# Three x loads on ScalarE's queue, squares behind the first roundings, small results turned inside block 3, and block 4 rounded ahead of the gates

## The chip, the cores and the metric

The kernel runs on one core of one Trainium2 chip. The metric is the time of one launch on the device in microseconds (us). The program computes a two-layer model on 256 tokens of width 1024. This case is about its first 40 us.

## What is computed

The part of the reference that the change touches is the first norm, the one large product after it, and what happens to the small columns of that product. The rest of the model (chunked attention of four kinds, feed-forward blocks, a second layer with differential attention) follows and is the same in both kernels.

```python
def rms_norm(x, g):
    xf = x.astype(jnp.float32)
    y = xf * lax.rsqrt(jnp.mean(xf * xf, axis=-1, keepdims=True) + EPS)
    return (y * g.astype(jnp.float32)).astype(x.dtype)

def token_mix(h, w_in, ...):                     # h = rms_norm(x, norm1_g)
    p = (h @ w_in).astype(jnp.float32)           # 1024 x 3612
    (fox_qkv, fox_f, gdn_qkv, gdn_b, gdn_a, gdn_z, hg_q, hg_f, hg_i, hg_g,
     gla_qk, gla_v, gla_gk, gla_g) = jnp.split(p, _cut_points(IN_SIZES), axis=-1)
    log_f = jax.nn.log_sigmoid(fox_f + fox_b_f).transpose(0, 2, 1)
    qkv = jax.nn.silu(causal_dwconv(gdn_qkv, gdn_conv_w))
    beta = jax.nn.sigmoid(gdn_b).transpose(0, 2, 1)
    g = (-jnp.exp(gdn_a_log) * jax.nn.softplus(gdn_a + gdn_dt_bias)).transpose(0, 2, 1)
    log_a = jax.nn.log_sigmoid(gla_gk @ gla_w_gk + gla_b_gk) / GLA_NORM
    ...
```

## The kernel before

**Tiling.** Activations stand channel-major: `x` is 128 partitions by 8 chunks of 128 channels by 256 tokens. All weights come as one stream of blocks of 1024 rows by 256 columns (1 MB each), into a ring of three slots, `raw`. Products are made in float32 precision from rounded parts: ScalarE rounds a block into `w_hi` (the helper `split`, called `block_hi(n)` here), VectorE writes the rest `raw - w_hi` into `w_lo` (`block_lo(n)`), and TensorE adds three products for each chunk: high by high, low weight by high operand, high weight by low operand. A block of 256 columns is therefore 48 products of 128x256, in two halves of 24 (`project(n, 0)` and `project(n, 1)`).

**Semaphores around the blocks.** `hi_ready` and `lo_ready` count rounded blocks, `raw_loaded0` to `2` the loads of a slot, `block_used` the blocks that TensorE is done with. SyncE's `weights_in(n)` waits for `lo_ready` of the block that last used the slot and issues the next load; `split` waits for the load and for `block_used`.

**The opening.** Block 0 holds the 28 small columns (gates of three heads groups and the low-rank input `gla_gk`), block 1 is `gdn_q`, block 2 `gdn_k`, block 3 `gdn_v`, block 4 `hg_q`, block 5 `fox_q`. SyncE issues all loads: for each of four quarters b the two x chunks (256 KB) and a quarter of block 1 (256 KB), with the small columns after the first; then block 2 in two halves, constants, `w_gk`, block 3, the row of biases, 1.6 MB of masks, block 4 and so on. ScalarE's `first_chunks` takes quarter by quarter: it rounds the weights (L1722), scales and rounds the two chunks into `h_hi` (L1725), and squares the two chunks (L1729). VectorE follows with the low parts (L2528, L2486), the small columns' low part (L2534), and the sums of the squares between them. TensorE warms up with 13 products of zeros (`keep_busy`), then `first_columns` does block 1 chunk by chunk, with the small columns two chunks behind: 72 products in all.

**The norm.** The products are made on the raw x; the reciprocal root `r_1` is multiplied in afterwards. `mean_of_x` is a product of ones with the summed squares, at once behind `first_columns`; ScalarE's `rstd_x` turns it into `r_1` (L1743, L1750). Then VectorE scales the small columns (L2547, `small_t`) and block 1 (L2604, `gdn_scale`). TensorE transposes the scaled small columns and multiplies by `w_gk` (`turn_small`, `gk_product`) between the halves of block 2.

**The convolution and the gates.** A gdn block is scaled by VectorE (`gdn_scale`), gets its last tap from ScalarE (`gdn_last_tap`, L1879) and three more from VectorE (`gdn_taps`, six of L2614). Gates: ScalarE copies the turned small columns (L1886) and rounds the masks (L1889), VectorE and ScalarE alternate over small tiles, and TensorE's `gates` sums them with the rounded masks behind block 3.

**What sets the order.** Every engine's program is written out by hand in one fixed order, and each queue runs in that order; nothing is scheduled at run time.

## Time and profile before

| | us |
|---|---|
| median of 3 runs | 1010.1 |
| lowest and highest | 1009.82 and 1011.12 |
| the profiled execution, whole | 1009.94 |
| its span in the profile | 1008.1 |
| TensorE busy in the span | 997.1 (99%) |
| VectorE, ScalarE, GpSimd busy | 848.4, 620.5, 9.5 |

A row of the timeline shows the start of a group of like instructions, the time from the first one's start to the last one's end, engine, source line, operation, tile written from tiles read, and in brackets how long the engine stood idle before it and what released it. A second row's start less the first's is what the first took of its engine's queue; that is used below as the pitch of an operation. Matmuls overlap, so their pitch (0.117 us for 128x256) is less than the length of one.

### The profile page before, as it was taken

Reading aid. Unit: us, or ns where it says so; the run is one execution under the profiler, and the core shown is the slowest. Engines: PE = TensorE matmul, PEld = TensorE weight load, DVE = VectorE, ACT = ScalarE, POOL = GpSimd, SP = SyncE. Lnnn points to the kernel's source line nnn. Section 1 sums busy time; section 2 is a strip of 40 time slices with the busy share of each in tenths; the row PEclk is TensorE's granted clock in tenths of the full one; section 3 lists DMA queues with packets and bytes.
Section 4 is the critical chain, followed back from the end, with each engine's and each line's share of the span. In section 5 each row is a group of like instructions: output and inputs, shape, how many; then the busy total and the mean of one; then the engine's idle time right before and its main releaser. Section 6 shows DMA issues by size and latency. Waiting matters only on the chain.

```text
span 1008.1 us, 20874 instructions
## 1 busy us (share of the span) xinstructions
PE 997.1 (99%) x8362; PEld 936.5 (93%) x8362; DVE 848.4 (84%) x1226; ACT 620.5 (62%) x858; POOL 9.5 (1%) x21
## 2 busy tenths in 40 slices
PE   8999999999999999999999999999999999999997
PEld 7999999999999998899999999999999999999996
DVE  5974896899988878879999888899776899988887
ACT  6754565657565655466666555775677676555575
POOL 0000001000000000001000000000000000000000
PEclk9999999999999999999999999999999999999999
DMA  9533315455655545566566554444444355655541
GB/s 330 179 124 97 126 44 201 165 192 187 208 190 184 196 143 204 180 235 210 199 209 209 174 203 171 165 165 170 165 147 152 126 204 205 212 178 196 184 150 42
DMA packets 26786, 177.04 MB, mean 176 GB/s; under 512 B 3261, under 2 KB 3541, under 8 KB 6368
## 3 DMA queue, kind: packets, MB, share of 16 engines
q1 hardware_dynamic: 25616, 171.31, 49.2%
q0 software_dynamic: 1104, 4.78, 1.6%
q8 instruction: 50, 0.82, 0.3%
q14 instruction: 16, 0.13, 0.0%
HBM read 175.02 MB, written 2.63 MB: 176 GB/s over the span
## 4 chain that ended last, share of the span: by engine, by line
PE 91%; DVE 4%; DMA 2%; ACT 2%; issue 1%; SPq 0%; DVEq 0%
PE PS L613 78%; PE PS L564 12%; DMA arena<-masks_in 1%; DVE w_lo L2473 1%; DMA raw<-weights 1%; DVE arena L2614 1%; DVE h_store L2486 0%; PE PS L1567 0%; DVE x L3158 0%; ACT w_hi L1662 0%; DVE arena L3390 0%; DVE arena L3152 0%; PE PS L935 0%; PE PS L903 0%; ACT arena L2043 0%
## 5 line engine op out<-in xcount | busy, mean ns | idle before, releaser
L613 PE MATMUL PS<-h_store,w_hi 128*128 128x256 f32 (+1 forms) x1840 | 475.5, 338 | 1.4 <-DVE w_lo L2528 1.2
L2473 DVE TENSOR_TENSOR w_lo<-raw,w_hi 128x2048 fp32r<-128x2048 f32 x152 | 347.9, 2290 | 50.6 <-ACT w_hi L1662 45.5
L613 PE MATMUL PS<-h_store,w_lo 128*128 128x256 f32 (+1 forms) x1400 | 365.4, 281 | 0.1
L1662 ACT ACTIVATE w_hi<-raw 128x2048 fp32r<-128x2048 f32 x154 | 294.2, 1911 | 82.6 <-PE PS L613 70.2
L613 PEld LDWEIGHTS PS<-h_store,w_hi 128*128 128x128 f32 x1840 | 303.6, 187 | 40.6 <-DVE w_lo L2528 1.7
L613 PEld LDWEIGHTS PS<-h_store,w_lo 128*128 128x128 f32 (+1 forms) x1400 | 253.2, 188 | 0.5 <-DVE h_store L3087 0.3
L613 PE MATMUL PS<-act_hi,w_hi 128*128 128x256 f32 x688 | 191.1, 280 | 0.2 <-DVE act_hi L3087 0.2
L613 PE MATMUL PS<-act_hi,w_lo 128*128 128x256 f32 x688 | 190.7, 279 | 0.1
L613 PE MATMUL PS<-act_lo,w_hi 128*128 128x256 f32 x688 | 187.6, 279 | 0.0
L613 PEld LDWEIGHTS PS<-act_hi,w_hi 128*128 128x128 f32 x688 | 129.3, 188 | 1.6 <-DVE act_hi L3087 0.6
L613 PEld LDWEIGHTS PS<-act_hi,w_lo 128*128 128x128 f32 x688 | 129.3, 188 | 0.3 <-DVE act_hi L3087 0.3
L613 PEld LDWEIGHTS PS<-act_lo,w_hi 128*128 128x128 f32 x688 | 127.5, 188 | 0.0
L2156 ACT ACTIVATE arena<-PS 128x512 f32<-128x512 f32 x51 | 30.2, 592 | 88.1 <-PE PS L613 88.1
L2148 ACT ACTIVATE arena<-arena,channel 128x256 f32<-128x256 f32 x132 | 63.6, 530 | 13.6 <-DVE arena L3235 12.4
L613 PE MATMUL PS<-w_hi,h_store 128*128 128x256 f32 (+1 forms) x368 | 71.3, 301 | 0.0
L3212 DVE SCALAR_TENSOR_TENSOR arena<-arena,channel 128x254 f32<-128x254 f32 x132 | 57.9, 480 | 7.6 <-DVE arena L3208 0.3
L613 PEld LDWEIGHTS PS<-w_hi,h_store 128*128 128x128 f32 x368 | 56.2, 188 | 2.9 <-ACT w_hi L1776 0.4
L3208 DVE SCALAR_TENSOR_TENSOR arena<-arena,channel 128x255 f32<-128x255 f32 x132 | 57.7, 479 | 1.0 <-ACT arena L2148 0.9
L3233 DVE TENSOR_TENSOR arena<-PS,arena 128x512 f32<-128x512 f32 x51 | 35.0, 686 | 20.9 <-ACT arena L2156 20.9
L613 PE MATMUL PS<-w_lo,h_store 128*128 128x256 f32 (+1 forms) x184 | 45.8, 296 | 0.4 <-DVE w_lo L2473 0.4
L564 PE MATMUL PS<-h_store,w_hi 128*128 128x256 f32 x256 | 45.4, 279 | 0.0
L564 PE MATMUL PS<-arena 64*64 64x64 f32 (+8 forms) x1356 | 41.5, 224 | 0.0
(405 smaller groups left out, 1147.1 us busy)
## 6 DMA issues: line engine op xcount, KB each, us to landing
raw<-weights SPq DMA_DIRECT2D x155, 1024.0 KB, 5.0
raw<-weights SPq DMA_DIRECT2D x12, 256.0 KB, 4.0
arena<-masks_in SPq DMA_DIRECT2D x1, 1600.0 KB, 12.2
bias_by_key<-bias_by_distance POOLq DMA_DIRECT2D x1, 1536.0 KB, 8.5
x<-x_in SPq DMA_DIRECT2D x4, 256.0 KB, 4.4
raw<-weights SPq DMA_DIRECT2D x2, 512.0 KB, 8.3
arena<-weights POOLq DMA_DIRECT2D x2, 512.0 KB, 6.1
arena<-bias_by_key POOLq DMA_DIRECT2D x1, 1024.0 KB, 6.6
```

The source lines that it names most:

```text
L564: return pe.matmul(o, lhs, rhs, start=start, stop=stop)
L613: return pe.matmul(o, lhs, rhs, start=start, stop=stop, skip_group_check=True)
L1662: act.activation(w_hi[:, slot, :], raw[:, slot, :], ACT.Copy).then_inc(hi_ready, 1)
L2148: ins = act.activation(dst[:, c, :], src[:, c, :], ACT.Identity, scale=w, bias=b)
L2156: act.activation(low, PS[:, bank:bank + 2, TOK:512], ACT.Copy).then_inc(sem("low_copied"), 1)
L2473: tt(w_lo[:, slot, :], raw[:, slot, :], w_hi[:, slot, :].bitcast(F), ALU.subtract).then_inc(lo_ready, 1)
L2614: mark(stt(dst, PS[:, bank_of_block(n), f * TOK:(f + 1) * TOK - d], ch("gdn_conv", (3 - d) * 6 + 2 * s + f), dst, ALU.mult, ALU.add))
L3208: stt(y[:, c, 1:TOK], src[:, c, 0:TOK - 1], channel[:, bass.ds(col(1) + c, 1)], y[:, c, 1:TOK], ALU.mult, ALU.add).then_inc(ready[0], 1)
L3212: ins = stt(y[:, c, 2:TOK], src[:, c, 0:TOK - 2], channel[:, bass.ds(col(0) + c, 1)], y[:, c, 2:TOK], ALU.mult, ALU.add)
L3233: tt(z, PS[:, bank:bank + 2, 0:TOK], low, ALU.add).then_inc(sem("parts_added"), 1)
```

## The change

1. **Loads.** SyncE still issues the first quarter of x. The other three are issued by ScalarE, behind its table load. The small columns are loaded behind the second weight quarter. The biases' row now counts on `ident_and_channel` (to 64), the masks alone on `mix_inputs` (to 16).
2. **Squares.** ScalarE squares the first half of x after the fourth quarter, and the second half after it has rounded block 2. VectorE's sums follow: one in front of block 2's low part, the rest behind it.
3. **First columns.** Of each chunk TensorE now does both high products, then both with the low weights, then both with the low operand, and waits for each kind by itself. The small results stand in bank 3 in place of 7.
4. **The mean** of the squares is taken inside the second half of block 2, the small columns are turned inside the first half of block 3, and `gates` moves behind the first half of block 4. Block 3 now does its low weights last, as blocks 2 and 4 to 7 did.
5. **ScalarE** rounds block 3 before `rstd_x`, and the second tap and block 4 before the masks and gates. **VectorE** takes block 3's low part ahead of the norm, scales blocks 1 and 2 together, and takes block 4's low part before the gates' arithmetic.

```diff
@@ SyncE @@
             sp.dma_start(channel[:, 0:KC], channel_in[:, 0:KC]).then_inc(sem("gains_loaded"), 16)
+            sp.dma_start(x[:, 0:2, :], x_in[:, 0:2, :]).then_inc(sem("x_loaded0"), 16)
             for b in range(4):
-                sp.dma_start(x[:, 2 * b:2 * b + 2, :], x_in[:, 2 * b:2 * b + 2, :]).then_inc(sem(f"x_loaded{b}"), 16)
...
-                if b == 0:
+                if b == 1:
                     sp.dma_start(raw[:, 0, 0:KC * SMALL], small_in).then_inc(raw_loaded[0], 16)
...
-            sp.dma_start(row[:, :], row_in.partition_broadcast(P)).then_inc(sem("mix_inputs"), 16)
+            sp.dma_start(row[:, :], row_in.partition_broadcast(P)).then_inc(sem("ident_and_channel"), 16)
@@ TensorE, first_columns @@
+                    pe.wait_ge(hi_chunk, k + 1)
+                    if k == 6:
+                        pe.wait_ge(hi_ready, 2)
...
+                    products(w_hi, h_hi, k == 0)
+                    if k == 6:
+                        pe.wait_ge(lo_ready, 2)
+                    elif k % 2 == 0:
+                        pe.wait_ge(sem("quarter_lo"), k // 2 + 1)
+                    products(w_lo, h_hi)
+                    pe.wait_ge(lo_chunk, k + 1)
+                    last = products(w_hi, h_lo, False, k == KC - 1)
@@ TensorE, project and its calls @@
-                low_last = n == 2 or 4 <= n <= 7
+                low_last = 2 <= n <= 7
...
             first_columns()
-            mean_of_x(0, 6, sum_1, True)
             project(2, 0)
-            turn_small()
-            gk_product()
-            project(2, 1)
-            project(3, 0)
+            project(2, 1, between=lambda: mean_of_x(0, 6, sum_1, True))
+            project(3, 0, between=small_parts)
             project(3, 1)
+            project(4, 0)
             gates()
-            project(4, 0)
             project(4, 1)
@@ ScalarE, first_chunks @@
-                    act.activation(sq4[:, b, :], flat(x[:, 2 * b:2 * b + 2, :]), ACT.Square).then_inc(sem("x_squares"), 1)
+                square(0)
+                square(1)
                 act.wait_ge(sem("half_loaded"), 16)
                 act.activation(w_hi[:, 2, 0:BLK // 2], raw[:, 2, 0:BLK // 2], ACT.Copy).then_inc(sem("quarter_hi"), 1)
                 act.wait_ge(raw_loaded[2], 16)
                 act.activation(w_hi[:, 2, BLK // 2:BLK], raw[:, 2, BLK // 2:BLK], ACT.Copy).then_inc(hi_ready, 1)
+                square(2)
+                square(3)
@@ ScalarE, order @@
             act.preload_act_table_set(TABLES)
+            for b in range(1, 4):
+                act.dma_start(x[:, 2 * b:2 * b + 2, :], x_in[:, 2 * b:2 * b + 2, :]).then_inc(sem(f"x_loaded{b}"), 16)
...
-            rstd_x(0, 6, (r_1, r_1_col))
...
             block_hi(3)
+            rstd_x(0, 6, (r_1, r_1_col))
             gdn_last_tap(0, 1)
+            small_copy()
+            gdn_last_tap(1, 2)
+            block_hi(4)
             gates()
             gk_logs()
-            block_hi(4)
-            gdn_last_tap(1, 2)
             block_hi(5)
@@ VectorE @@
-                if b == 2:
-                    sum_of_three(0, sum_1)
-            sum_of_last(0, sum_1)
-            fold_sum(sum_1)
+            dve.wait_ge(sem("x_squares"), 2)
+            link(tt(sum_1, sq4[:, 0, :], sq4[:, 1, :], ALU.add))
...
+            dve.wait_ge(sem("x_squares"), 3)
+            link(tt(sum_1, sum_1, sq4[:, 2, :], ALU.add))
+            sum_of_last(0, sum_1)
+            fold_sum(sum_1)
+            split(3, 3 % RING)
             dve.wait_ge(sem("x_rstd"), 1)
...
             gdn_scale(0, 1)
-            block_lo(3)
+            gdn_scale(1, 2)
+            gdn_taps(0, 1)
             gates_in()
-            gdn_taps(0, 1)
             gk_logits()
+            block_lo(4)
             gates()
             gate_parts()
             gk_logs()
-            gdn_scale(1, 2)
-            block_lo(4)
             gdn_taps(1, 2)
```

The order of instructions shows two places that matter. The first is ScalarE's queue at the opening; in it `w_hi<-raw` of 128x512 is a weight quarter, `h_store<-x` the operand, `xn<-x` a square. Before:

```order
L1857 ACT_TABLE_LOAD
L1722 ACTIVATE w_hi<-raw 128x512
L1725 ACTIVATE h_store<-x,channel 128x256 x2
L1729 ACTIVATE xn<-x 128x512
L1722 ACTIVATE w_hi<-raw 128x512
L1725 ACTIVATE h_store<-x,channel 128x256 x2
L1728 ACTIVATE w_hi<-raw 128x224
L1729 ACTIVATE xn<-x 128x512
```

And with the change:

```order
L1870 ACT_TABLE_LOAD
L1872 DMA x<-x_in 128x512 x3
L1732 ACTIVATE w_hi<-raw 128x512
L1735 ACTIVATE h_store<-x,channel 128x256 x2
L1732 ACTIVATE w_hi<-raw 128x512
L1735 ACTIVATE h_store<-x,channel 128x256 x2
L1738 ACTIVATE w_hi<-raw 128x224
L1732 ACTIVATE w_hi<-raw 128x512
```

The squares have left the gaps between the quarters, and three loads stand in front of everything that ScalarE computes.

The second place is VectorE between the small columns' scaling (`arena<-PS,xn` of 28 rows) and the low part of block 4 (`w_lo<-raw,w_hi` of 128x2048). Before, where block 3's low part is the third row and block 4's stands further on, behind the gates' arithmetic and the second block's scaling:

```order
L2547 TENSOR_TENSOR arena<-PS,xn 28x256
L2604 TENSOR_TENSOR PS<-PS,xn 128x512
L2473 TENSOR_TENSOR w_lo<-raw,w_hi 128x2048
L2558 TENSOR_TENSOR arena<-arena,row 128x16
L2614 SCALAR_TENSOR_TENSOR arena<-PS,channel,arena 128x255 x2
L2614 SCALAR_TENSOR_TENSOR arena<-PS,channel,arena 128x254 x2
L2614 SCALAR_TENSOR_TENSOR arena<-PS,channel,arena 128x253 x2
L2586 TENSOR_TENSOR arena<-PS,row 128x2x128
L2563 SCALAR_TENSOR_TENSOR arena<-arena 128x8
```

And with the change:

```order
L2490 TENSOR_TENSOR w_lo<-raw,w_hi 128x2048
L2567 TENSOR_TENSOR arena<-PS,xn 28x256
L2624 TENSOR_TENSOR PS<-PS,xn 128x512 x2
L2634 SCALAR_TENSOR_TENSOR arena<-PS,channel,arena 128x255 x2
L2634 SCALAR_TENSOR_TENSOR arena<-PS,channel,arena 128x254 x2
L2634 SCALAR_TENSOR_TENSOR arena<-PS,channel,arena 128x253 x2
L2578 TENSOR_TENSOR arena<-arena,row 128x16
L2606 TENSOR_TENSOR arena<-PS,row 128x2x128
L2490 TENSOR_TENSOR w_lo<-raw,w_hi 128x2048
L2583 SCALAR_TENSOR_TENSOR arena<-arena 128x8
```

Block 3's low part stands ahead of the wait for the norm, block 2's scaling beside block 1's, and block 4's low part ahead of the gates' small tiles.

## Rows read from the trace of the kernel before

**Rows 1.** The page: span, busy us of engines, a group's busy and mean ns.
```profile
span 1008.1 us, 20874 instructions
...
PE 997.1 (99%) x8362; PEld 936.5 (93%) x8362; DVE 848.4 (84%) x1226; ACT 620.5 (62%) x858; POOL 9.5 (1%) x21
...
L1662 ACT ACTIVATE w_hi<-raw 128x2048 fp32r<-128x2048 f32 x154 | 294.2, 1911 | 82.6 <-PE PS L613 70.2
```

**Rows 2.** TensorE's waits, 0 to 100 us: engine, tile, releaser, us, times, longest.
```profile
PE PS L613 <- DVE w_lo L2528: 1.2, 3, 0.8
```

**Rows 3.** The same view from 85 us to the end, its longest.
```profile
PE PS L613 <- ACT xn L2335: 0.2, 1, 0.2
```

**Rows 4.** ScalarE's timeline: start, us, line, tiles, idle before.
```profile
6.00 0.63 ACT L1722 ACTIVATE w_hi<-raw 128x512 fp32r<-128x512 f32 x1 [3.97 <-DMA raw<-weights]
...
7.33 0.61 ACT L1729 ACTIVATE xn<-x 128x512 f32<-128x512 f32 x1
8.48 0.63 ACT L1722 ACTIVATE w_hi<-raw 128x512 fp32r<-128x512 f32 x1 [0.53 <-DMA raw<-weights]
...
21.67 0.81 ACT L1879 ACTIVATE arena<-PS,channel 128x256 f32<-128x256 f32 x2
```

**Rows 5.** TensorE's timeline, 0 to 43 us.
```profile
1.51 5.71 PE L613 MATMUL PS<-zeros_r 128*128 128x512 f32 x13 [1.51 <-POOL zeros_r L524]
...
11.08 0.28 PE L613 MATMUL PS<-h_store,w_hi 128*28 128x256 f32 x1 [0.21 <-DVE w_lo L2534]
...
14.95 0.35 PE L613 MATMUL PS<-h_store,w_hi 128*128 128x256 f32 x1 [0.21 <-DVE w_lo L2528]
...
17.81 0.59 PE L613 MATMUL PS<-arena,ones 128*128 128x256 f32 x2
...
25.29 0.39 PE L613 MATMUL PS<-h_store,w_hi 128*128 128x256 f32 x2
...
30.89 0.28 PE L564 MATMUL PS<-arena,level_masks 128*128 128x8 f32 x2
...
39.85 1.21 PE L613 MATMUL PS<-w_lo,h_store 128*128 128x256 f32 x8 [0.42 <-DVE w_lo L2473]
```

**Rows 6.** SyncE's timeline: issue of block 1's second quarter.
```profile
3.09 0.43 SPq L463 DMA_DIRECT2D raw<-weights  x1
```

**Rows 7.** DMA issues at 3.0 to 3.5 and 14.8 to 14.9 us: KB, us to landing.
```profile
raw<-weights SPq DMA_DIRECT2D x1, 256.0 KB, 5.4
...
raw<-weights SPq DMA_DIRECT2D x1, 1024.0 KB, 11.7
```

**Rows 8.** Windows: busy of PE, PEld, DVE, ACT, POOL; granted clock, DMA share, GB/s.
```profile
2.00:4.00 2.00, 2.00 (x6) 1.52 (x6) 0.00 (x0) 0.03 (x1) 0.00 (x0) 1.00 0.82 132
...
6.00:8.00 2.00, 1.81 (x9) 1.19 (x8) 1.34 (x3) 1.95 (x4) 0.00 (x0) 1.00 0.97 335
```

**Rows 9.** VectorE's timeline, 19 to 40 us.
```profile
19.99 0.41 DVE L2547 TENSOR_TENSOR arena<-PS,xn 28x256 f32<-28x256 f32 x1 [1.07 <-ACT xn L1750]
...
24.41 2.68 DVE L2614 SCALAR_TENSOR_TENSOR arena<-PS,channel,arena 128x255 f32<-128x255 f32 x6
27.37 0.42 DVE L2586 TENSOR_TENSOR arena<-PS,row 128x256 f32<-128x256 f32 x1 [0.27 <-DVE arena L2614]
27.71 0.16 DVE L2563 SCALAR_TENSOR_TENSOR arena<-arena 128x8 f32<-128x8 f32 x1
...
29.96 0.69 DVE L2604 TENSOR_TENSOR PS<-PS,xn 128x512 f32<-128x512 f32 x1
...
33.20 2.68 DVE L2614 SCALAR_TENSOR_TENSOR arena<-PS,channel,arena 128x255 f32<-128x255 f32 x6
36.59 0.17 DVE L2598 TENSOR_TENSOR arena<-arena 128x8 f32<-128x8 f32 x1 [0.72 <-DVE arena L2614]
36.91 0.70 DVE L2604 TENSOR_TENSOR PS<-PS,xn 128x512 f32<-128x512 f32 x1
37.52 2.28 DVE L2473 TENSOR_TENSOR w_lo<-raw,w_hi 128x2048 fp32r<-128x2048 f32 x1
```

More of the change, by code:

```diff
@@ L961, in small_products, with products @@
                     if k == KC - 1:
-                        last.then_inc(block_used, 1)
+                        last.then_inc(block_used, 2)
                 for k in range(KC):
-                    if k % 2 == 0 and k < 6:
-                        pe.wait_ge(sem("quarter_lo"), k // 2 + 1)
-                    for lo in range(2):
-                        pe.wait_ge(lo_chunk if lo else hi_chunk, k + 1)
-                        if k == 6 and lo == 0:
-                            block_ready(1)
-                        a = h_lo if lo else h_hi
+                    pe.wait_ge(hi_chunk, k + 1)
+                    if k == 6:
+                        pe.wait_ge(hi_ready, 2)
+                    def products(w, a, first=False, final=False):
                         for f in range(2):
                             at = slice(k * 256 + f * P, k * 256 + (f + 1) * P)
-                            o = PS[:, 5, f * TOK:(f + 1) * TOK]
-                            last = add(o, w_hi[:, 1, at], a[:, k, :], k == 0 and f == 0 and lo == 0, k == KC - 1 and lo == 1)
-                            if lo == 0:
-                                add(o, w_lo[:, 1, at], a[:, k, :])
+                            ins = add(PS[:, 5, f * TOK:(f + 1) * TOK], w[:, 1, at], a[:, k, :], first and f == 0, final)
+                        return ins
+                    products(w_hi, h_hi, k == 0)
[6 more added lines that the diff above has]
+                    last = products(w_hi, h_lo, False, k == KC - 1)
                     if k >= 2 and k < KC - 1:
@@ L1000, in exact, with project @@
                 return level_masks[:, MASK[name], :]
-            def project(n, f, ks=range(KC)):
+            def project(n, f, ks=range(KC), between=None):
                 slot, bank = n % RING, bank_of_block(n)
-                low_last = n == 2 or 4 <= n <= 7
+                low_last = 2 <= n <= 7
                 if f == 0 and ks[0] == 0:
@@ L1014, in project @@
                 if low_last:
-                    last = project_by_part(n, f, slot, bank)
+                    last = project_by_part(n, f, slot, bank, between)
                 for k in () if low_last else ks:
@@ L1031, in project, with project_by_part @@
                     last.then_inc(block_used, 1)
-            def project_by_part(n, f, slot, bank):
+            def project_by_part(n, f, slot, bank, between):
                 channel_major = MIX_ORDER[n] in CHANNEL_MAJOR
@@ L1046, in project_by_part @@
                     product(w_hi, h_lo, k, False, False)
+                    if between is not None and k == 3:
+                        between()
                 if f == 0:
@@ L1714, in first_chunks, with square @@
             def first_chunks():
+                def square(b):
+                    act.activation(sq4[:, b, :], flat(x[:, 2 * b:2 * b + 2, :]), ACT.Square).then_inc(sem("x_squares"), 1)
                 for b in range(4):
@@ L1881, in gdn_last_tap, with small_copy @@
                 ins.then_inc(sem("gdn_last_tap"), 1)
-            def gates():
-                act.wait_ge(sem("mix_inputs"), 32)
+            def small_copy():
                 act.wait_ge(sem("small_turned"), 1)
@@ L1887, in gates @@
                     .then_inc(once("small_ready")[0], 1)
+            def gates():
+                act.wait_ge(sem("mix_inputs"), 16)
                 act.activation(level_masks[:, :, :], masks[:, 0:N_LEVEL_MASKS, :], ACT.Copy) \
```

16 lines of the change are left out of this document (9 added, 7 removed).

## The prediction

> **What bounds the kernel now.** Read the page first: TensorE is busy for 997.1 us of a span of 1008.1 us [rows 1], so no edit that keeps its instructions can bring more than its waits. Then its waits: in the first 100 us it waits 1.2 us for quarters of `w_lo` (L2528) and 0.42 us for block 5's `w_lo` (L2473) [rows 2, 5]; after 85 us the longest is 0.2 us [rows 3]. Then the timelines of the opening, where the change lies. It adds and removes no matmul. The question is only how much earlier or later TensorE gets through the last wait of the opening, the one for block 5's low part at 39.85 us [rows 5]. From there each engine's order is the old one, nothing there waits for the clock on the wall, and I let the rest follow with the same shift. The sum is made against the profiled execution, 1009.94 us; the median is 0.16 us above it.
>
> **Before, as a sum.** The small columns' first product starts at 11.08 us, 2.60 us after ScalarE began the second quarter at 8.48 [rows 4, 5]. From it on TensorE has 54 products until the mean of squares. A product's pitch is 0.117: the 48 of block 3 stand between 25.29 and 30.89 [rows 5]. So 54 x 0.117 = 6.30 us, which would end at 17.38; the mean starts at 17.81 [rows 5], and the 0.43 between are one stall, ended by the fourth quarter's low part at 14.95 [rows 5]. From 17.81 to 39.85 are 22.04 us, of which 0.42 are the wait for block 5; TensorE's own work there is 21.62.
>
> **Part 1, the stall at the fourth quarter: gone, -0.43.** VectorE no longer sums squares ahead of that quarter, ScalarE no longer squares (0.61 us each [rows 4]) between quarters, and TensorE starts each chunk with products that need no low part. The 54 products run through as long as the third quarter starts on ScalarE within 2.7 us of the second and the fourth within 5.0. Write s for the start of the second quarter; the first columns end at F = s + 2.60 + 6.30 = s + 8.90. The finer waits gain nothing more, for the first small product waits for the small low part, which VectorE makes last of its quarter as before.
>
> **Part 2, the loads: +0.3.** ScalarE's first quarter costs 1.33 us without its square (6.00 to 7.33), and the second starts at 8.48 only because its weights land then: issued at 3.09, landed 5.4 later [rows 4, 6, 7]. Is that issue or data? In 2 to 4 us the 16 DMA engines are 0.82 busy, in 6 to 8 us 0.97 busy at 335 GB/s [rows 8]. So it is data. Before, 1136 KB stood in the queue up to and with that quarter (two of x, two of weights, the small columns). Now at least 1024 KB must land; 112 KB less is 0.34 us at 335 GB/s, so s is 8.1 at best. But the second half of x now comes through another queue at the same time: if both queues get equal shares, 1536 KB land first, 400 KB more, 1.2 us, so s is 9.7 at worst. I take 8.8, a little under the middle, because SyncE's first two loads start before ScalarE's, which stand behind its table load. The first quarter may slip by up to 1.2 us too, to 7.2; with 1.33 behind it that is 8.5, under 8.8, and costs nothing. Then F = 17.70.
>
> Equal shares are my end of a range from byte counts; no row of before has two queues. The Trainium skill, DMA: Bandwidth & Descriptors, Queues, rings and completion order, says that a DMA engine goes round-robin between queue rows, packet by packet, which is that worse end. Its section Issuing engines are not separate DMA queues says that issuing from several engines saves only issue time, so it speaks against this edit. The trace agrees so far as the DMA engines were full.
>
> **Part 3, the squares and the mean: hidden.** ScalarE starts the second quarter at 8.8; three quarters of 1.33, the small columns, two squares of 0.61 and block 2 (1.91 for a block [rows 1]) put its end of block 2 at 16.3, or 16.8 if the later loads hold it by half a microsecond: before F at 17.7. Two more squares and VectorE's three sums, of the same size as its scaling of 0.7 [rows 9], end by about 20. TensorE asks for them 24 + 8 products behind F, at F + 3.74 = 21.4. That cover is over 1 us.
>
> **Part 4, what waits for the norm is late: +0.11.** This is the price of moving the mean. The small columns' scaling started 2.18 us after the mean (17.81 to 19.99 [rows 5, 9]). Now it starts at F + 3.74 + 2.18 = F + 5.92 in place of F + 2.18. It takes with it VectorE's whole chain to block 5's low part. Step by step, in pitches from [rows 4, 9]: small scaling 0.34; block 1's scaling 0.68 and ScalarE's two taps 0.81 with two hand-overs of 0.05 (block 2's scaling, 0.61, lies under them), 1.93 so far; six taps 2.96 (24.41 to 27.37); gates' input 0.09; the low-rank logits 0.34; block 4's low part 2.22; gates, their parts and logs 2.10 (27.71 to 29.96 less a wait of 0.15); block 2's taps 3.39 (33.20 to 36.59); 0.32 and 0.61 to block 5; its low part 2.28. Sum 16.24. It ends at F + 22.16. TensorE without any wait would be there at F + 21.62, so it waits 0.54 where it waited 0.42, and goes on at F + 22.15 or so. Block 3's low part (2.2) has left this chain, which pays most of the 3.74. Queued behind that wait on TensorE are block 5's low products, the transposes of q and k, and all else.
>
> **Hidden as well.** Turning the small columns inside block 3 needs the scaling at F + 6.3; TensorE is there at F + 7.5. Block 4 has to be rounded by F + 11.2 = 28.9 for VectorE. ScalarE is free at about F + 8.7 (two pairs of taps of 0.81 behind the scaling), its load landed before at 14.83 + 11.7 = 26.5 [rows 7], and 1.91 us of rounding ends at 28.4; that is half a microsecond of cover. If the cover is gone, each microsecond of lateness goes into the wait for block 5. The masks are rounded behind it, ready 2 us before TensorE's gates. Moving the row's semaphore costs nothing: the row is issued ahead of the masks as before.
>
> **The sum.** Before, TensorE goes on at 17.81 + 22.04 = 39.85. After, at 17.70 + 22.15 = 39.85. The change is 0.0 us: the time is that of before, which I put at 1010.0, between the profiled execution and the median.
>
> **Rivals.**
> 1. *The queues share evenly.* The full DMA engines speak for it [rows 8], ScalarE's later start against. s = 9.5, F = 18.4, on at 40.55: +0.7, so 1010.7. This is what the Trainium skill's round-robin rule (DMA: Bandwidth & Descriptors, Queues, rings and completion order) would do here.
> 2. *Issue time was the limit after all.* The second weight quarter is issued 0.9 us earlier (two issues fewer ahead of it on SyncE, of 0.43 us each [rows 6]) and lands so much earlier: s = 7.6, F = 16.5, on at 38.65: -1.2, so 1008.7. For it: in 2 to 4 us only 132 GB/s moved [rows 8], so two queues may fill a slow start. Against it: the 0.97 share after.
> 3. *VectorE's chain is shorter than added up*, by overlaps that I count twice. TensorE then never waits for block 5: F + 21.62, at F = 17.70 on at 39.3: -0.5, so 1009.4. With rival 2 it would be -1.7.
> 4. *Slower: TensorE's clock falls.* It warms up with 13 zero products at 0.44 us for 512 columns [rows 5], twice the 0.234 that the pitch of 0.117 for 256 gives, so at 1.2 GHz for most of 5.7 us, and 2.4 GHz after. They end at 7.2; the first real product would now start near 8.1 in place of 7.4, with thin work until 11.4. If the clock fell there and took another 5.3 us of steady work to return, that work would take 2.7 us longer: 1012.7. It decides at the gap between the zeros and the first product. Against it: gaps of 0.8 us before left the column at 1.00 [rows 2, 8].
> 5. *Block 3 or block 4 lands late*, over 0.5 us, since the loads' order has changed: +0.5 to +1.5, 1011.0.
>
> **How the numbers follow.** Forecast 0.47, rival 1 0.17, rival 2 0.14, rival 3 0.12, rival 4 0.04, rival 5 0.06. A measurement of this kernel tells 0.2%, 2.0 us, from no change. Of these only rival 4 and a corner of rival 5 are slower by that: 0.05. Only rivals 2 and 3 together come near it on the fast side: 0.05. Within 0.2%: 0.90. The range takes rivals 1, 2, 3 and most of 5, that is 1008.4 to 1011.4; the ends of s alone (8.1 and 9.7) give 1009.3 to 1010.9, and VectorE's chain is good to half a microsecond.
>
> **What would show it.** ScalarE's second quarter starts near 8.8; no stall of TensorE between the first small product and F; F near 17.7, with no mean behind it; the small scaling near 23.6 in place of 19.99; TensorE's wait for `w_lo` before block 5's low products about 0.5 us, ending near 39.9. A second quarter before 8.0 or after 9.8, a wait for block 2, 3 or 4's low part, or a block 5 that is on before 39 or after 41 would prove the forecast wrong.

## The result, and the profile after

| | before | changed |
|---|---|---|
| median, us (20 runs each, same chip) | 1010.15 | 1012.01 |
| lowest and highest | 1009.56 to 1012.09 | 1010.72 to 1013.36 |
| profiled execution, whole | 1009.94 | 1013.36 |
| its span | 1008.1 | 1011.6 |

The medians differ by 1.86 us. The ratio is 1.0014 with a 95% interval of 1.0008 to 1.0020: slower than before, by a part that lies under the 0.2% that the prediction set as its bound, but clear of 1. The median is 0.6 us above the range's upper end (1011.4). The profiled execution is the slowest of the twenty, so the sizes read from it are the upper side of what happens.

The page of the changed kernel, to be held against [rows 1]:

```profile
span 1011.6 us, 20869 instructions
PE 998.5 (99%) x8362; PEld 938.5 (93%) x8362; DVE 848.0 (84%) x1226; ACT 620.4 (61%) x858; POOL 9.4 (1%) x21
PEclk8999999999999999999999999999999999999999
```

TensorE is busy 1.4 us longer with the same 8362 matmuls, and the rest of the 3.5 us by which its span grew is waiting. ScalarE's timeline of the opening:

```profile
0.75 1.28 ACT L1870 ACT_TABLE_LOAD   x1 [0.75 <-PEq L3768]
0.78 1.37 ACTq L1872 DMA_DIRECT2D x<-x_in  x3
8.44 0.63 ACT L1732 ACTIVATE w_hi<-raw 128x512 fp32r<-128x512 f32 x1 [6.41 <-DMA raw<-weights]
8.97 0.90 ACT L1735 ACTIVATE h_store<-x,channel 128x256 fp32r<-128x256 f32 x2
9.77 0.61 ACT L1732 ACTIVATE w_hi<-raw 128x512 fp32r<-128x512 f32 x1
```

The three loads are issued at 0.78, beside the table load and not behind it. The first weight quarter, which ScalarE began at 6.00 before [rows 4], is there at 8.44. The second is begun 1.33 us later without any wait: it had landed in the meantime. TensorE's timeline, with the first product, the mean of squares and block 5's low products:

```profile
1.50 5.03 PE L613 MATMUL PS<-zeros_r 128*128 128x512 f32 x13 [1.50 <-POOL zeros_r L524]
9.52 0.80 PE L613 MATMUL PS<-h_store,w_hi 128*128 128x256 f32 x2 [2.99 <-ACT h_store L1735]
...
20.68 2.15 PE L613 MATMUL PS<-h_store,w_hi 128*28 128x256 f32 x17
...
24.54 0.59 PE L613 MATMUL PS<-arena,ones 128*128 128x256 f32 x2
...
43.22 1.22 PE L613 MATMUL PS<-w_lo,h_store 128*128 128x256 f32 x8 [0.82 <-DVE w_lo L2490]
```

In the row at 20.68 one product of the small columns and block 2's first 16 stand together; the second one starts at 20.80, 3.74 us (32 products) ahead of the mean. So F, the end of the first columns, is 20.80; it was 17.81 [rows 5], and 17.70 was forecast. TensorE goes on with block 5 at 43.22 in place of 39.85 [rows 5], 3.37 us later. From there to the end of the span are 968.4 us (1011.6 less 43.2), and before 968.3: the whole difference is made in the first 43 us, as the prediction assumed. Between the zeros and the first product TensorE stood still for 2.99 us. What followed is in the windows (TensorE, its weight loads, VectorE, ScalarE, GpSimd, then the granted clock, the DMA engines' share and GB/s):

```profile
2.00:4.00 2.00, 2.00 (x6) 1.52 (x6) 0.00 (x0) 0.03 (x1) 0.00 (x0) 1.00 0.74 202
6.00:8.00 2.00, 0.53 (x3) 0.10 (x1) 0.00 (x0) 0.00 (x0) 0.00 (x0) 1.00 1.03 294
8.00:10.00 2.00, 0.48 (x2) 0.48 (x3) 0.90 (x2) 1.56 (x4) 0.00 (x0) 0.70 1.07 415
10.00:12.00 2.00, 2.00 (x11) 2.00 (x11) 2.00 (x6) 2.00 (x6) 0.00 (x0) 0.50 1.02 411
14.00:16.00 2.00, 2.00 (x13) 1.91 (x12) 1.76 (x4) 2.00 (x4) 0.00 (x0) 0.60 0.86 348
16.00:18.00 2.00, 2.00 (x20) 1.93 (x19) 1.80 (x2) 2.00 (x4) 0.00 (x0) 1.00 0.79 263
```

The granted clock is at half, 1.2 GHz of 2.4, from 8.8 to 15.6 us. A product's pitch is 0.213 us there and 0.117 after.

Last, what the two queues carried from 2 to 4 us and from 4 to 6 us; q10 is ScalarE's, q1 SyncE's (packets, MB, share of the engines). First 2 to 4, then 4 to 6:

```profile
DMA packets 307, 0.40 MB, mean 202 GB/s; under 512 B 111, under 2 KB 111, under 8 KB 307
q10 hardware_dynamic: 148, 0.28, 52.3%
q1 hardware_dynamic: 159, 0.13, 21.6%
```

```profile
q1 hardware_dynamic: 170, 0.32, 50.6%
q10 hardware_dynamic: 170, 0.31, 43.9%
```

The numbers of packets are near each other in both stretches, the bytes only in the second. Of the 159 packets of SyncE's queue from 2 to 4 us, 99 are under 512 B; most of these belong to the 4 KB of gains (`channel`), which stand at its head as 128 packets of 32 B. The gains' issue to landing, before and with the change:

```profile
channel<-channel_in SPq DMA_DIRECT2D x1, 4.0 KB, 1.8
```

```profile
channel<-channel_in SPq DMA_DIRECT2D x1, 4.0 KB, 3.2
```

They were issued at 0.75 us in both kernels, so they landed at 2.58 and at 3.95 us, and the first x quarter stands behind them. The trace also has the landing of each of the 16 parts that a load is made of. Of the 32 parts of the first pair (x and weights), 24 had landed by 5.28 us before and by 6.83 with the change, the last one at 5.89 and at 8.33. So some 1.5 us of the delay fell on most parts, and 0.9 more on the last ones.

### The profile page after: what moved, and what is told of

It is laid out like the page before. It is cut to its first block, busy times and chain, and to the rows that moved or that the text cites. A ratio compares the mean times of both kernels' runs of the same rounds, so it can differ in the third digit from the quotient of the medians.

```text
span 1011.6 us, 20869 instructions
## 1 busy us (share of the span) xinstructions
PE 998.5 (99%) x8362; PEld 938.5 (93%) x8362; DVE 848.0 (84%) x1226; ACT 620.4 (61%) x858; POOL 9.4 (1%) x21
## 4 chain that ended last, share of the span: by engine, by line
PE 93%; DVE 4%; ACT 2%; issue 1%; DMA 1%; DVEq 0%; SPq 0%; ACTq 0%
PE PS L613 79%; PE PS L564 12%; DVE w_lo L2490 1%; DMA raw<-weights 1%; DVE arena L2634 1%; PE PS L1574 0%; DVE h_store L2503 0%; DVE x L3177 0%; DVE arena L3409 0%; DVE arena L3171 0%; PE PS L935 0%; PE PS L903 0%; ACT arena L2058 0%; DVE arena L3043 0%; ACT arena L1860 0%
```

## The experiments

The theory after the result: the loads alone carry the loss, first by making the opening's first tile late, then by giving TensorE a pause after which its clock can fall. Against it stood these rivals: the moved squares, mean or roundings cost something too; the clock is all of it; the bytes ahead in the queue are not what counts, since any second queue makes the first pair land late (C in the expectations). R is the time at which TensorE goes on with block 5's low products. All ratios are to the kernel before on the same chip. "Low" counts the runs whose granted clock over the whole span was 0.997 or less; of the kernel before's runs beside these experiments 2 of 108 are, of the changed kernel's first twenty 17. It is a sign and no count of falls: half the clock for 6.8 us takes 0.0034 off the share, and a shorter fall can go unseen.

| run | median us | before | ratio, 95% | low |
|---|---|---|---|---|
| loads undone | 1010.01 | 1010.38 | 0.9994, 0.9985 to 1.0003 | 1 of 11 |
| loads alone | 1011.64 | 1010.38 | 1.0012, 1.0003 to 1.0021 | 9 of 11 |
| zeros longer | 1011.22 | 1010.38 | 1.0008, 0.9999 to 1.0017 | 0 of 11 |
| pairs | 1011.38 | 1010.38 | 1.0012, 1.0003 to 1.0021 | 4 of 11 |
| zeros shorter | 1009.96 | 1009.96 | 0.9996, 0.9987 to 1.0006 | 3 of 11 |
| block 5's low part first | 1011.01 | 1009.96 | 1.0009, 1.0000 to 1.0018 | 0 of 11 |
| small columns second | 1009.99 | 1009.96 | 0.9997, 0.9987 to 1.0006 | 0 of 11 |
| one x load | 1010.32 | 1009.96 | 0.9998, 0.9989 to 1.0007 | 3 of 11 |
| no zeros | 1010.20 | 1010.29 | 0.9998, 0.9989 to 1.0007 | 0 of 11 |
| first columns alone | 1010.11 | 1010.29 | 0.9999, 0.9990 to 1.0008 | 1 of 11 |
| changed kernel again | 1011.56 | 1010.44 | 1.0013, 1.0004 to 1.0022 | 8 of 11 |
| zeros longer, again | 1011.25 | 1010.44 | 1.0007, 0.9998 to 1.0016 | 0 of 11 |

### The loads undone, and the loads alone

The changed kernel with its loads as before:

```diff
-            sp.dma_start(x[:, 0:2, :], x_in[:, 0:2, :]).then_inc(sem("x_loaded0"), 16)
             for b in range(4):
+                sp.dma_start(x[:, 2 * b:2 * b + 2, :], x_in[:, 2 * b:2 * b + 2, :]).then_inc(sem(f"x_loaded{b}"), 16)
...
-                if b == 1:
+                if b == 0:
                     sp.dma_start(raw[:, 0, 0:KC * SMALL], small_in).then_inc(raw_loaded[0], 16)
...
-            for b in range(1, 4):
-                act.dma_start(x[:, 2 * b:2 * b + 2, :], x_in[:, 2 * b:2 * b + 2, :]).then_inc(sem(f"x_loaded{b}"), 16)
```

> The changed kernel with its loads as before (all on SyncE, small columns behind the first weight quarter); everything else of the change stays. Theory A (the loads cost the time: the first weight quarter lands at 8.3 us in place of 5.9, and the 3.0 us gap before the first product lets TensorE's clock fall): the second quarter starts at 8.5 us, first columns end near 17.4, TensorE goes on with block 5 near 39.8, no fall of the clock, 1010.1 us, within 0.5 of before. Rival B (the moved mean and VectorE's longer wait cost it): 1011 to 1012 us, with the wait for block 5's low part over 1.5 us.

The other one is the kernel before with the same lines the other way round.

> The kernel before with the loads of the change alone (x's last three quarters on ScalarE's queue, small columns behind the second weight quarter). Theory A: ScalarE's first quarter starts near 8.4 us, its second near 10.3 (squares are between them again), the clock falls in most runs; 1012 to 1013 us, as slow as the whole change or slower. Rival B: 1010.1 us, as before.

Undone, the time is 1010.01 and the loss is gone, as Theory A had it. Alone, 1011.64 brings it back, though a little less than the 1012 to 1013 of the forecast; the second quarter started at 10.03 us. ScalarE's timeline with the loads undone, with both quarters waiting for their own data, close to [rows 4]:

```profile
5.88 0.63 ACT L1732 ACTIVATE w_hi<-raw 128x512 fp32r<-128x512 f32 x1 [3.85 <-DMA raw<-weights]
...
8.37 0.63 ACT L1732 ACTIVATE w_hi<-raw 128x512 fp32r<-128x512 f32 x1 [1.06 <-DMA raw<-weights]
```

TensorE in the same kernel:

```profile
10.96 0.28 PE L613 MATMUL PS<-h_store,w_hi 128*28 128x256 f32 x1 [0.29 <-DVE w_lo L2549]
...
20.98 0.59 PE L613 MATMUL PS<-arena,ones 128*128 128x256 f32 x2
...
39.66 1.21 PE L613 MATMUL PS<-w_lo,h_store 128*128 128x256 f32 x8 [0.79 <-DVE w_lo L2488]
```

No row between 10.96 and 39.66 has a wait of its own. From the first small product to F (20.98 less 3.74, 17.24) are 6.28 us, the prediction's 54 pitches; the stall of [rows 5] is gone. F is 0.57 earlier than before, R only 0.19: the later norm takes most of it back, as Part 4 says.

With the loads alone:

```profile
1.51 5.03 PE L613 MATMUL PS<-zeros_r 128*128 128x512 f32 x13 [1.51 <-POOL zeros_r L524]
9.58 0.58 PE L613 MATMUL PS<-h_store,w_hi 128*128 128x256 f32 x1 [3.04 <-DVE w_lo L2530]
...
20.78 0.59 PE L613 MATMUL PS<-arena,ones 128*128 128x256 f32 x2
...
42.49 1.21 PE L613 MATMUL PS<-w_lo,h_store 128*128 128x256 f32 x8
```

The same pause of 3.04 us, the clock at half from 8.76 to 15.59, and R at 42.49, 2.64 late. No other edit is needed for the loss, and none of the others adds to it measurably.

### More zeros

The changed kernel, with warm-up products until the real ones can start, so that the pause goes and the late loads stay:

```diff
-            keep_busy(13, 4)
+            keep_busy(25, 4)
```

> The changed kernel with 25 warm-up products of zeros in place of 13: at 0.22 us each at the full clock they end near 9 us, where the first real product can start. Theory A with the clock as the larger half: the clock stays at 1.00 through the first columns, their pitch is 0.117 from the start, they end near 18.7 in place of 20.8; 1010.9 us, about 1.1 under the changed kernel. If the late load alone costs the time and the clock nothing: 1012.0 us.

> The changed kernel with 25 warm-up products of zeros, once more, beside the changed kernel itself. If the fallen clock is a cost on top of the late load: 1011.1 us, about 0.8 under the changed kernel, and no run above 1012. If the late load is all: the same time as the changed kernel.

1011.22 and 1011.25, each 0.8 above the kernel before beside it, though both intervals touch 1. None of the 22 runs has a low clock. TensorE, first run:

```profile
1.50 8.25 PE L613 MATMUL PS<-zeros_r 128*128 128x512 f32 x25 [1.50 <-POOL zeros_r L524]
...
21.75 0.59 PE L613 MATMUL PS<-arena,ones 128*128 128x256 f32 x2
...
40.42 1.21 PE L613 MATMUL PS<-w_lo,h_store 128*128 128x256 f32 x8 [0.79 <-DVE w_lo L2490]
```

R is 40.42 here and 40.34 in the second run: 0.5 to 0.6 behind the kernel before and 0.7 to 0.8 behind the one with its loads undone. That is the loads' lateness without the clock; the second quarter started at 9.08 and 8.93 us in these two profiles. The medians' share for the clock is the rest, and it is known only roughly. The changed kernel's 31 runs have a median of 1011.9, these 22 one of 1011.24, 0.7 us apart, but the 31 were not all taken beside the 22. Side by side on one chip, 11 runs each, the medians are 1011.56 and 1011.25, 0.3 us apart, less than either kernel's own scatter. The second expectation missed twice: it had 0.8 us between the two, and no run above 1012, where the highest was 1012.6 and its clock shows no fall. What makes such a run slow is not shown, for one run of each kernel alone has a trace.

### The changed kernel again

> The changed kernel itself once more, beside the next one on the same chip, so that the share of the clock can be read from two times taken together. 1012.0 us, with runs between 1010.7 and 1013.4.

1011.56. Eight of its eleven runs have a low clock (their median is 1011.78), the three others 1011.19. The profiled one is of the three:

```profile
9.26 0.50 PE L613 MATMUL PS<-h_store,w_hi 128*128 128x256 f32 x2 [3.15 <-ACT h_store L1735]
...
12.16 0.28 PE L613 MATMUL PS<-h_store,w_hi 128*28 128x256 f32 x1 [0.27 <-DVE w_lo L2551]
...
22.20 0.59 PE L613 MATMUL PS<-arena,ones 128*128 128x256 f32 x2
...
40.88 1.22 PE L613 MATMUL PS<-w_lo,h_store 128*128 128x256 f32 x8 [0.79 <-DVE w_lo L2490]
```

```profile
10.00:12.00 2.00, 1.90 (x15) 1.69 (x14) 2.00 (x6) 2.00 (x6) 0.00 (x0) 1.00 1.02 412
```

It is the same program with a pause of 3.15 us and a clock that stays at 1.00. F is 18.46 and R 40.88. Against the first profile (43.22) R is 2.34 earlier, of which 0.26 is the second quarter (9.51 for 9.77). The rest, 2.1 us, is what one fall of the clock cost here, where it covered the dense products of the first columns.

### One queue for x, the other for the weights

The changed kernel with all x on SyncE's queue and the four weight quarters on ScalarE's, so that within each queue the quarters stand in order of use, with the small columns behind the first x quarter again:

```diff
             for b in range(4):
-                quarter = slice(b * BLK // 4, (b + 1) * BLK // 4)
-                sp.dma_start(raw[:, 1, quarter], weights[0][:, quarter]) \
-                    .then_inc(sem(f"x_loaded{b}") if b < 3 else raw_loaded[1], 16)
+                sp.dma_start(x[:, 2 * b:2 * b + 2, :], x_in[:, 2 * b:2 * b + 2, :]).then_inc(sem(f"x_loaded{b}"), 16)
...
-            for b in range(1, 4):
-                act.dma_start(x[:, 2 * b:2 * b + 2, :], x_in[:, 2 * b:2 * b + 2, :]).then_inc(sem(f"x_loaded{b}"), 16)
+            for b in range(4):
+                quarter = slice(b * BLK // 4, (b + 1) * BLK // 4)
+                act.dma_start(raw[:, 1, quarter], weights[0][:, quarter]) \
+                    .then_inc(sem(f"x_loaded{b}") if b < 3 else raw_loaded[1], 16)
```

> The changed kernel with all of x back on SyncE and block 1's four weight quarters on ScalarE's queue, so that the two queues carry the two halves of each pair at the same time. Theory A (queues share the DMA engines evenly, what matters is what is asked for first): the first pair lands near 5.9 us as before, the second near 8; first columns end near 17, no fall of the clock, 1009.7 us. Rival C (any second queue at the opening slows the first pair): the first quarter starts after 7.5 us and the time is 1011 to 1012 us.

1011.38, as slow as the loads alone. ScalarE:

```profile
0.78 1.85 ACTq L1870 DMA_DIRECT2D raw<-weights  x4
7.04 0.63 ACT L1729 ACTIVATE w_hi<-raw 128x512 fp32r<-128x512 f32 x1 [5.01 <-DMA x<-x_in]
...
9.36 0.63 ACT L1729 ACTIVATE w_hi<-raw 128x512 fp32r<-128x512 f32 x1 [0.88 <-DMA x<-x_in]
```

The first weight quarter is issued 0.9 us earlier than in the kernel before, its x at the same time, and the pair lands a microsecond later (C named 7.5 us or more for the start, and it was 7.04; its time of 1011 to 1012 us came true). The second pair is 0.9 late. By the sums, the rate is not the cause: from 4 to 6 us 232 GB/s moved, where the profile with one queue (loads undone) has 318, but from 2 to 4 us it was 207 for 143, and up to 6 us the sums are close, 0.88 MB for 0.92. It is a question of whose bytes they were. By 5.9 us ScalarE's queue had moved 0.54 MB, as much as the first two weight quarters, and SyncE's 0.32 MB, little more than the first x quarter (0.26), which had waited behind the gains as in the changed kernel (95 of SyncE's 154 packets from 2 to 4 us are under 512 B). The pair's last part landed at 6.93. So order within each queue does not keep the pairs in order, for nothing holds the two queues in step. That the gains' small packets are what put SyncE's queue behind is read from the traces; no run moved them.

### One x load alone on ScalarE's queue

```diff
             for b in range(4):
+                if b in (1, 2):
+                    sp.dma_start(x[:, 2 * b:2 * b + 2, :], x_in[:, 2 * b:2 * b + 2, :]).then_inc(sem(f"x_loaded{b}"), 16)
...
-            for b in range(1, 4):
+            for b in range(3, 4):
                 act.dma_start(x[:, 2 * b:2 * b + 2, :], x_in[:, 2 * b:2 * b + 2, :]).then_inc(sem(f"x_loaded{b}"), 16)
```

> The changed kernel with only the last quarter of x on ScalarE's queue, in place of three. Theory A (the queues share evenly, so what the first pair loses is what the other queue holds, 256 KB in place of 768): the first weight quarter is used near 6.8 us in place of 8.4, the gap in front of the first product is about 1.3 us, the clock stays up, 1010.5 us. Rival C (the mere use of a second queue slows the opening): 7.7 us or later and 1011.5 to 1012 us.

The median, 1010.32, sides with the count of bytes; the profiled run does not. There the first quarter starts at 7.56 in place of the forecast 6.8, and the clock falls after a pause of only 1.79 us:

```profile
8.64 0.50 PE L615 MATMUL PS<-h_store,w_hi 128*128 128x256 f32 x2 [1.79 <-ACT h_store L1737]
```

That run took 1011.44, others as little as 1009.55. The landings explain the 7.56: of the first pair's 32 parts 31 had landed by 5.94 us, about as before, and the last one at 7.45. So the first pair as a whole is hardly late, and the quarter waits for one straggling part. By the medians one load costs nothing that these runs can tell; how often such a straggler comes, one profile does not say.

### Fewer zeros, and none

On the kernel before, with its loads untouched: is a pause enough to cost time?

```diff
-            keep_busy(13, 4)
+            keep_busy(7, 4)
```

> The kernel before with 7 warm-up products in place of 13, nothing else: they end near 4.5 us, so TensorE stands idle for nearly 3 us before its first real product at 7.4, as long as in the changed kernel, while all loads stay as they were. Theory A (the clock is a cost of its own): the clock is at 0.5 through most of the first columns, their end moves from 17.8 to about 20, 1012 us. If the clock costs nothing by itself: 1010.2 us.

```diff
-            keep_busy(13, 4)
+            keep_busy(0, 4)
```

> The kernel before without its 13 warm-up products, nothing else, so that TensorE's clock is low at its first real product in every run and not only in some; all loads as before. Theory A (a low clock at the opening costs by itself, where the loads are on time): the first columns' products go at 0.21 us a piece until the clock rises after some 5 us of work, the first columns end near 19.5 in place of 17.8, TensorE is through block 5's wait near 41.1, 1011.3 us, 1.1 above before. If a low clock is hidden by the data's pace: 1010.1 us.

Theory A missed in both; the times fit the other branch of each, 1010.2 and 1010.1. With 7 zeros the clock is low in 3 of 11 runs only, and the median is 1009.96. In the profiled run it did fall, after a pause of 2.39 us, for 6.8 us; the mean of squares starts 1.52 us late (19.33), R only 1.19 (41.04). With no zeros the pitch is 0.213 until 13.3 us in the profile, the mean starts at 18.52, 0.71 late, and R at 40.23, 0.38 late; the time is 1010.20 beside 1010.29:

```profile
18.52 0.59 PE L613 MATMUL PS<-arena,ones 128*128 128x256 f32 x2
...
40.23 1.21 PE L613 MATMUL PS<-w_lo,h_store 128*128 128x256 f32 x8
```

What took up 0.33 us in both is a wait that the prediction does not name. In the kernel before, ScalarE copies the small columns only when the masks have landed:

```profile
24.07 0.22 ACT L1886 ACTIVATE arena<-PS 128x56 f32<-128x56 f32 x1 [1.59 <-DMA arena<-masks_in]
```

VectorE waits for that copy and starts its gates at 24.32. With 7 zeros it starts them at 25.52 and with none at 24.71, 1.20 and 0.39 later, without a wait, and R is later by 1.19 and 0.38. So slow products in the first microseconds hide in part behind the data's own pace, and a further 0.3 us of them behind the masks. The zeros are worth nothing that shows here. The fall cost 2.1 us at F in the changed kernel and 1.5 with 7 zeros; that in the changed kernel the data had piled up before TensorE started is the likely reason, and was not tested.

### Block 5's low part first

The loads undone, and the wait of 0.79 us attacked on VectorE:

```diff
             gdn_taps(1, 2)
+            block_lo(5)
             gate_products()
             gdn_scale(2, 3)
-            block_lo(5)
             gdn_taps(2, 3)
```

> The changed kernel with its loads on SyncE as before (as e1), and VectorE's low part of block 5 ahead of the gates' products and the scaling of block 3. It aims at TensorE's wait of 0.8 us for that low part. Theory A (after the loads that wait is what is left of the opening): the wait is gone, TensorE goes on near 38.9 in place of 39.7, no new wait behind it, 1009.3 us. Rival D (the moved scaling makes the transposes of v late and the wait comes back behind block 5): 1010.0 us, with a wait of TensorE near 44 us.

1011.01, 1 us over the kernel that it was made from, though on another chip. R is 38.94, with no wait. Then:

```profile
38.94 1.21 PE L613 MATMUL PS<-w_lo,h_store 128*128 128x256 f32 x8
...
44.41 0.63 PE L1069 MATMUL PS<-ident,arena 128*128 128x128 f32 x4 [0.55 <-ACT arena L1940]
...
47.76 1.21 PE L613 MATMUL PS<-w_lo,h_store 128*128 128x256 f32 x8 [0.83 <-DVE w_lo L2488]
```

The wait came back as two, 0.55 for the tile whose taps VectorE now made later, and 0.83 for block 6's low part. D in the expectations had the first of them, but not the second, and so 1 us too little time: TensorE goes on behind block 6's low products at 48.81, where with the loads undone it is 47.69. In this stretch VectorE sets the pace, and moving one of its results forward made two others late.

### The small columns behind the second weight quarter

The loads undone, all on SyncE, and this one moved:

```diff
-                if b == 0:
+                if b == 1:
                     sp.dma_start(raw[:, 0, 0:KC * SMALL], small_in).then_inc(raw_loaded[0], 16)
```

> The changed kernel with its loads on SyncE as before but the small columns behind the second weight quarter, where the change puts them. 112 KB fewer stand in front of the second quarter. If data rate decides: the second quarter starts on ScalarE near 8.1 in place of 8.4 us and all moves by 0.3 us, 1009.7 us. If stragglers among the 16 engines decide: 8.4, 1010.0 us.

1009.99, equal to before. The second quarter starts at 8.22 for 8.37, and R is 39.53 for 39.66. By these two profiles its 112 KB are worth 0.15 us, not the 0.34 that bytes by rate gave, and the two differ by less than landings do from run to run.

### The new order of the first columns alone

The kernel before, with the new order of change 3 and VectorE's sums behind the fourth quarter:

```diff
+                    products(w_hi, h_hi, k == 0)
+                    if k == 6:
+                        pe.wait_ge(lo_ready, 2)
+                    elif k % 2 == 0:
+                        pe.wait_ge(sem("quarter_lo"), k // 2 + 1)
+                    products(w_lo, h_hi)
+                    pe.wait_ge(lo_chunk, k + 1)
+                    last = products(w_hi, h_lo, False, k == KC - 1)
...
-                if b == 2:
-                    sum_of_three(0, sum_1)
+            sum_of_three(0, sum_1)
             sum_of_last(0, sum_1)
```

> The kernel before with two pieces of the change alone: the new order of products and waits in the first columns, and the sums of squares on VectorE behind all of the fourth quarter. Loads, mean, norm, gates and blocks 3 and 4 stay as before. Theory A (the one real gain of the change is the stall of 0.43 us at the fourth quarter, and the moved mean gives most of it back): that stall is gone, the mean starts near 17.4 in place of 17.8, TensorE goes on with block 5 near 39.4, 1009.7 us; too little for the timing to tell, so the profile decides. If the sums now come late: a wait of TensorE ahead of the mean and 1010.3 us.

1010.11, no change. The stall is gone here too: from the first small product at 11.43 to the mean at 17.73 are 6.30 us. R does not follow, it is 1.01 later than before and far from the forecast 39.4. The sums are not to blame: VectorE scales the small columns at 19.91, where it was 19.99. ScalarE's wait for the masks is, which ends at 25.08 in place of 24.07:

```profile
25.08 0.22 ACT L1891 ACTIVATE arena<-PS 128x56 f32<-128x56 f32 x1 [2.68 <-DMA arena<-masks_in]
```

```profile
40.86 1.22 PE L613 MATMUL PS<-w_lo,h_store 128*128 128x256 f32 x8 [0.63 <-DVE w_lo L2478]
```

From the end of that wait to R are 15.78 us in both kernels. This profiled run (1011.21) is one of the slower ones; its second quarter started at 8.83. So in the kernel before R hangs on the masks as soon as they land late. The changed kernel, which rounds block 4 ahead of the masks, has no such wait in its two profiles.

## Why the prediction was wrong where it was

**Part 1, the stall, -0.43: right.** 6.28 us from the first small product to F, with the loads undone.

**Part 2, the loads, +0.3: wrong, and the step that failed.** Three statements of it fell.
- "I take 8.8 ... because SyncE's first two loads start before ScalarE's, which stand behind its table load." They were issued at 0.78 us, during the table load (0.75 to 2.03), and so ahead of SyncE's first x. The doubt should have gone to the other end: s was 9.77, and 9.51 in the second profile, where 9.5 was rival 1's value. The Trainium skill, DMA: Bandwidth & Descriptors, Queues, rings and completion order, has the round-robin by packet, and the 170 packets against 170 of 4 to 6 us agree with it, and nearly so the 148 against 159 of 2 to 4 us.
- "The first quarter may slip by up to 1.2 us too, to 7.2 ... and costs nothing." It slipped by 2.4 (2.2 in the second profile). The argument counted bytes up to the second quarter and gave the first one the same slip. But the first pair is 512 KB, and equal shares put 512 KB of the other queue beside it, not 400: 1.5 us at 335 GB/s, by the prediction's own rule, so a start at 7.5, which with 1.33 behind it is already past 8.8. The rest, 0.7 to 0.9 us, is no sum of bytes: from 2 to 4 us the shares were 0.28 MB for ScalarE's queue to 0.13 for SyncE's, and the last parts of the quarter straggled. With the first at 8.2 to 8.4, the second could not start before 9.5.
- "If both queues get equal shares, 1536 KB land first, 400 KB more, 1.2 us, so s is 9.7 at worst." For the second quarter's own landing the bound held, it was 9.02 and 8.76 us. But s was 9.77, for the first quarter set it, and there the worst end is not equal shares of bytes: the traces show near equal numbers of packets, and a queue with small packets at its head gets fewer bytes. Nor does a sum of bytes hold how far the last part is behind the others.

**Rivals 1 and 4, priced as if they excluded each other.** The profile of the changed kernel with a full clock is rival 1 almost to the number: F 18.46 for 18.4, R 40.88 for 40.55. Rival 4's point of decision, the gap between the zeros and the first product, was right, but the gap was put at 0.85 us and was 3.0. Of that difference 1.4 us follow from the late first quarter (the first product at 9.52 for 8.1), so that the one case brings the other with it; the other 0.7 come from the zeros, which ended at 6.5 us and not at 7.2. Its price was 2.7 and measured 2.1 in one profile; since the clock does not fall in every run, it is worth 0.3 to 0.7 at the median. The late loads without the clock were 0.8 over the kernel before in the two kernels with longer zeros. Together that is 1.1 to 1.5 us. Measured were 1.86 in the first twenty runs and 1.12 in the second set; the 0.4 to 0.7 by which the first is larger are not accounted for.

**Part 3, squares and mean: right.** TensorE has no wait at the mean in any profile of the changed kernel. Block 4, which the prediction hid behind half a microsecond of cover, is rounded in time too: VectorE takes its low part at 32.23 without a wait.

**Part 4, the late norm, +0.11: right in kind, 0.27 short.** VectorE's small scaling and block 5's low part in the changed kernel:

```profile
26.71 0.41 DVE L2567 TENSOR_TENSOR arena<-PS,xn 28x256 f32<-28x256 f32 x1 [1.41 <-ACT xn L1763]
...
40.88 2.28 DVE L2490 TENSOR_TENSOR w_lo<-raw,w_hi 128x2048 fp32r<-128x2048 f32 x1
```

The first starts at F + 5.91 (forecast 5.92). The second ends at 43.16, so the chain takes 16.45 us for the 16.24 added up. The wait is 0.82 for 0.54, and R is F + 22.42 for F + 22.15; with the loads undone and in the second profile it is again 22.42. Rival 3, a shorter chain, did not happen. The 22.04 of before, against which this is held, has the 0.33 us of the masks in it: where VectorE does not wait for them, R is F + 21.71 with the old order (loads alone, 7 zeros, no zeros). So by these rows the late norm itself costs 0.7 us, and taking the masks out of the way gives 0.3 back; the prediction has neither number.

**Rival 2, issue time: wrong.** The weights' issues moved 0.9 us forward and the landings of the first two weight quarters moved back, to 8.33 from 5.89 and to 9.02 from 8.46. What came earlier was not needed yet: x's second quarter landed at 4.45 in place of 6.7. Two queues did fill the slow start, with 202 GB/s for 132 from 2 to 4 us, but mostly with such bytes. The Trainium skill, DMA: Bandwidth & Descriptors, Issuing engines are not separate DMA queues, says that only issue time is saved; the traces agree in so far as the saved 0.9 us brought the first pair nothing.

**The end.** With the loads undone the sum by what was measured is -0.43 for the stall, +0.38 for the late norm (22.42 for 22.04) and -0.11 for a second quarter that started at 8.37 and not 8.48; R moved by -0.19, and the time by less than these runs can tell. Without the second quarter's 0.11, the parts other than the loads moved R by -0.08, where -0.32 was forecast (-0.43 and +0.11). Both are too small for the times to tell.

What stays open: why the granted clock falls after one pause of 3 us and not after another, what makes single parts of a load straggle by 1 us and more, and whether the first pair would come on time if the gains' small packets did not stand ahead of it.

## What to carry to other kernels

Loads on which the first tile depends stay in one queue, in the order in which they are used. A second queue shares the DMA engines from its first packet on, and what it carries early can come out of the time of the tile that is needed first: three x loads on it cost this kernel 1.1 to 1.9 us, one x load nothing that could be told. Where two queues do run, look at what stands at the head of each: they took turns by the packet here, and the x quarter behind 4 KB in packets of 32 B fell behind the other queue. When two rivals share a cause (here a late first tile, which also opens a pause in TensorE's work), add them up in one case instead of giving each a chance of its own. And bound a delay at the first consumer that can see it, not at the one on which the sum was built.

## What the runs showed of the hardware

- DMA issues of ScalarE's queue do not wait for its table load: they stand at 0.78 us, the load at 0.75 to 2.03.
- Two queues got about equal numbers of packets, 148 and 159 from 2 to 4 us and 170 and 170 from 4 to 6. The bytes were 0.28 and 0.13 MB in the first stretch, where 99 of the one queue's 159 packets were under 512 B, and 0.31 and 0.32 in the second.
- The gains' 4 KB landed at 2.3 to 2.6 us in the profiles with one queue and at 3.6 to 4.2 in those with two.
- The last part of a load can be far behind the others: the 32nd of the first pair's 32 parts landed at 7.45 us, the 31st at 5.94 (one x load).
- By the sign used in the table, the clock fell in 17 of 20 and 8 of 11 runs of the same program. In the profiles it fell in or just after pauses of 2.99, 3.04, 2.39 and 1.79 us, and not with pauses of 3.15 (changed kernel again) and 1.93 (pairs). In the first three of these it stayed at half for 6.8 us, in the fourth for 3.4.
- The column of the granted clock does not tell the clock of an engine that has not yet warmed up. Without zeros the pitch was 0.213 us until 13.3, and the column reads full:

```profile
10.00:12.00 2.00, 2.00 (x11) 1.85 (x11) 1.67 (x4) 2.00 (x5) 0.00 (x0) 1.00 0.96 275
```
